# A first stage by channels: x scaled by g alone on ScalarE, its rows loaded beside the first weights

## The reference, cut to what matters

```python
def mixer_layer(h, mix_norm_g, w_in, ...):
    hn = rms_norm(h, mix_norm_g)
    proj = hn @ w_in            # h: 16 meta tokens, then x: 1024 tokens of 1024 channels
    rq, rk, rv, rg, sq, sk, sv, gr, gs = jnp.split(proj, split_points, axis=-1)
    ...
    return merged @ w_out
...
h = h + mixer_layer(h, ...)
hn = rms_norm(h, mlp_norm_g[layer])
h = h + jnp.square(jax.nn.relu(hn @ w_up[layer])) @ w_down[layer]
```

## Time and profile before

| | |
|---|---|
| median of three runs | 1614.77 us (1614.22 to 1615.44) |
| the profiled execution | 1615.03 us, its span 1613.1 us |
| PE / DVE / ACT / POOL busy | 1603.3 / 1038.1 / 769.6 / 425.7 us |
| DMA over the span | 157 GB/s |

### The profile page before, as it was taken

The page is one execution under the profiler, slowest core; times in us unless marked ns, Lnnn a source line. Parts: engine busy times, 40 slices in busy tenths (PEclk is TensorE's granted clock), DMA queues, the critical chain, the costliest instruction groups (busy, mean ns, idle before and its releaser), DMA issues.

```text
span 1613.1 us, 22668 instructions
## 1 busy us (share of the span) xinstructions
PE 1603.3 (99%) x7984; PEld 1340.3 (83%) x7984; DVE 1038.1 (64%) x1977; ACT 769.6 (48%) x1567; POOL 425.7 (26%) x611
## 2 busy tenths in 40 slices
PE   8999999999999999999999999999999999999999
PEld 6888888888888888888888888888888888888887
DVE  6775556655657787766554338866665656766675
ACT  6533334544547777762122126655555544444442
POOL 1001010221238898874211000122112222100000
PEclk9999999999999999999999999999999999999999
DMA  8323231645436566668553223354444389633452
GB/s 282 125 97 117 98 124 66 239 149 190 163 110 159 158 176 167 159 159 267 167 187 111 66 78 118 126 174 151 144 144 155 120 316 358 240 96 98 153 180 92
DMA packets 128815, 253.31 MB, mean 157 GB/s; under 512 B 14928, under 2 KB 50176, under 8 KB 128704
## 3 DMA queue, kind: packets, MB, share of 16 engines
q1 hardware_dynamic: 82656, 124.81, 24.8%
q0 software_dynamic: 45904, 126.93, 23.5%
q10 hardware_dynamic: 144, 0.13, 0.0%
HBM read 157.05 MB, written 69.47 MB: 140 GB/s over the span
## 4 chain that ended last, share of the span: by engine, by line
PE 93%; DMA 2%; DVE 2%; POOL 1%; ACT 1%; issue 0%; SPq 0%; DVEq 0%; ACTq 0%
PE bank L1089 29%; PE bank L1094 28%; PE bank L1093 28%; PE bank L1375 2%; PE bank L1407 1%; PE bank L1389 1%; DMA RT<-YA 1%; DMA XCH<-in_x_ch 0%; POOL PR L966 0%; PE bank L1132 0%; PE bank L1507 0%; PE bank L1293 0%; PE bank L1424 0%; PE bank L1457 0%; DVE WL L2177 0%; PE bank L1411 0%
## 5 line engine op out<-in xcount | busy, mean ns | idle before, releaser
L1089 PE MATMUL bank<-WH,ADH 128*128 128x512 f32 x448 | 174.3, 389 | 0.0
L1093 PE MATMUL bank<-WH,ADL 128*128 128x512 f32 x448 | 174.3, 389 | 0.0
L1094 PE MATMUL bank<-WL,ADH 128*128 128x512 f32 x448 | 174.3, 389 | 0.0
L1089 PE MATMUL bank<-HN,WH 128*128 128x512 f32 x384 | 152.9, 398 | 0.1
L966 POOL TENSOR_SCALAR PR<-PR,RC 128x272 f32<-128x272 f32 (+1 forms) x128 | 139.3, 1228 | 47.4 <-DVE RC L2672 47.2
L2103 ACT CAST ADH<-ARAW 128x512 fp32r<-128x512 f32 x112 | 69.5, 621 | 169.9 <-PE bank L1094 156.7
L1094 PE MATMUL bank<-HN,WH 128*128 128x512 f32 x384 | 150.2, 391 | 0.0
L1093 PE MATMUL bank<-HN,WL 128*128 128x512 f32 x384 | 150.1, 391 | 0.0
L2926 DVE TENSOR_TENSOR ADL<-ARAW,ADH 128x512 fp32r<-128x512 f32 x112 | 77.5, 692 | 97.1 <-ACT ADH L2103 97.1
L1089 PE MATMUL bank<-SOPH,WH 128*128 128x512 f32 x256 | 99.8, 390 | 0.0
L1093 PE MATMUL bank<-SOPH,WL 128*128 128x512 f32 x256 | 99.6, 389 | 0.0
(11 more groups left out here) (356 smaller groups left out, 4200.6 us busy)
## 6 DMA issues: line engine op xcount, KB each, us to landing
ARAW<-uop SPq DMA_DIRECT2D x112, 256.0 KB, 3.1
uop<-US POOLq DMA_DIRECT2D x64, 256.0 KB, 2.8
WRAW<-in_w_up SPq DMA_DIRECT2D x15, 1024.0 KB, 6.3
PW<-PR SPq DMA_DIRECT2D x56, 272.0 KB, 3.0
RAW<-in_w_in SPq DMA_DIRECT2D x58, 256.0 KB, 4.1
gates<-TB POOLq DMA_DIRECT2D x48, 256.0 KB, 2.7
uop<-UA POOLq DMA_DIRECT2D x48, 256.0 KB, 3.2
proj<-SA POOLq DMA_DIRECT2D x36, 256.0 KB, 2.5
```

The costliest lines, as they stand in the source:

```text
L1089: mm = pe.matmul(bank, ahi, bhi, start=first, stop=False, skip_group_check=onto)
L1093: pe.matmul(bank, alo, bhi, start=False, stop=False, skip_group_check=onto)
L1094: return pe.matmul(bank, ahi, blo, start=False, stop=last, skip_group_check=onto)
```

## The change

The first stage is rebuilt. Each norm factor belongs to a token, so it can be applied to the product's rows instead of to x. Blocks 0, 1 and 2 (FIRST = 3) now go to PE as x's channels times g alone: ACT scales four tiles of 128x128 into XGH (`hi_xg`, an activation with g as scale per partition), DVE makes the low part XGL from XCH, g and XGH (`lo_xg`), and the factor comes in when the finished bank is copied (`evict_first`, scale = RSTD). Blocks 0 and 1 share PE in pairs of steps, block 2 follows, then 3 to 7 as before. All eight blocks are still scaled for HN and SR, in the order SEQ = 3, 4, 5, 6, 7, 0, 1, 2, for which the channels of blocks 0 to 2 are loaded a second time. The eight transposes of g, `keep_x` and the transposes of blocks 0 and 1 are gone. Factor rows stand after the steps given in ROWS. The squares go in the order STAT. The loads of x's rows are all POOL's, the first four as soon as the first high part is made (`pool.wait_ge(hn_hi, 1)`); g's load goes to ACT's queue, and SP loads halves of x's channels of blocks 0 and 1 between the weights. The first sums follow the loop.

```diff
+FIRST = 3
+SEQ = (3, 4, 5, 6, 7, 0, 1, 2)
+STAT = (3, 4, 0, 5, 1, 2, 6, 7, NB)
...
         # SP
+            LATE_XG = {1: (1, 0), 3: (0, 1), 4: (1, 1)}
+            load_xg(0, 0)
             load_slab(0, w_cols(w_in, 0))
+            sp.dma_start(XCH[:, 2, :, :], x_ch[2]).then_inc(xc_full[2], 16)
+            for p in range(NB):
+                if p < 3:
+                    sp.wait_ge(hn_lo, max(XG_AT[p, 0], XG_AT[p, 1]))
+                else:
+                    sp.wait_ge(xs_rdy, 2 * (p - 2))
+                sp.dma_start(XCH[:, p % 3, :, :], x_ch[SEQ[p]]).then_inc(xc_full[p % 3], 16)
             sp.dma_start(GBC[0:META, :], g_mix[0:META, :]).then_inc(g_full, 16)
...
         # POOL
-            pool.wait_ge(w_ready, 3)
-            load_x(2)
+            pool.wait_ge(hn_hi, 1)
+            for i in range(4):
+                load_x(i)
             pool.dma_start(COLS[:, :, :], c_cols[:, 0:4 * HR].rearrange("p (a h) -> p a h", a=4)).then_inc(c_full, 16)
...
+            load_x(4)
+            load_x(5)
             store_rq(0)
+            load_x(6)
+            store_rq(1)
             load_x(7)
-            store_rq(1)
+            store_rq(2)
             load_x(8)
...
         # PE
+            keep_warm(4)
+            for pair in range(KT // 2):
+                for b in range(2):
+                    for k in (2 * pair, 2 * pair + 1):
+                        first_step(b, k)
+            ROWS = {(2, 1): 0, (3, 0): 1, (3, 5): 2, (4, 3): 3, (5, 1): 4, (5, 6): 5, (6, 4): 6, (7, 2): 7}
+            for b in range(2, NB):
+                if b == 4:
+                    pe.wait_ge(a_free, 1)
+                elif b > 4:
+                    pe.wait_ge(a_free, b - 1)
+                for k in range(KT):
+                    first_step(b, k)
+                    if (b, k) in ROWS:
+                        factors_row(ROWS[b, k])
+                    if (b, k) == (6, 6):
+                        transpose_meta()
+            pe.wait_ge(hn_lo, lo_at(1, 1))
...
         # ACT
+            def hi_xg(b, u):
+                if u == 0 or b < 2:
+                    act.wait_ge(xg_full(b, u), 16)
+                if (b, u) == XG_SEQ[0]:
+                    act.wait_ge(gc_full, 16)
+                for k in range(4 * u, 4 * u + 4):
+                    hi = act.activation(XGH[:, b, k, :], XCH[:, b, k, :], ACT.Copy, scale=GCH[:, k:k + 1])
+                hi.then_inc(hn_hi, 1)
...
+            hi_xg(0, 0)
             split_hi(0, 0, first=True)
             split_hi(0, 1, first=True)
+            hi_xg(1, 0)
+            split_hi(0, 2, first=True)
+            split_hi(0, 3, first=True)
+            hi_xg(0, 1)
+            split_hi(0, 4, first=True)
+            hi_xg(1, 1)
             for k in range(5, KT):
                 split_hi(0, k, first=True)
+            hi_xg(2, 0)
+            hi_xg(2, 1)
+            square_x(0)
+            square_x(1)
+            hi_x(3)
+            square_x(2)
+            evict_first(0)
+            square_x(3)
+            hi_x(4)
+            square_x(4)
+            evict_first(1)
+            square_x(5)
+            evict_first(2)
+            hi_x(5)
+            square_x(6)
+            evict_first(3)
+            hi_x(6)
+            square_x(7)
+            evict_first(4)
+            hi_x(7)
+            square_x(8)
+            evict_first(5)
+            hi_x(0)
+            hi_meta()
+            hi_x(1)
+            evict_first(6)
+            for k in range(4):
+                st_hi(0, 0, k)
+            hi_x(2)
+            evict_first(7)
...
         # DVE
+            def lo_xg(b, u):
+                dve.wait_ge(hn_hi, XG_AT[b, u])
+                for k in range(4 * u, 4 * u + 4):
+                    lo = dve.scalar_tensor_tensor(out=XGL[:, b, k, :], in0=XCH[:, b, k, :], scalar=GCH[:, k:k + 1],
+                                                  in1=XGH[:, b, k, :].bitcast(F32), op0=ALU.mult, op1=ALU.subtract)
+                lo.then_inc(hn_lo, 1)
...
+            invert(3)
+            dve.wait_ge(raw_full[3], 32)
+            factors(3)
+            for p in range(NB):
+                scale_x(p)
+                if p == 2:
+                    invert(2)
+                if p < 4:
+                    invert(SEQ[p + 1])
+                if p < NB - 1:
+                    factors(SEQ[p + 1])
+                lo_x(SEQ[p])
+                if p < 2:
+                    invert(p)
+                elif p == 4:
+                    invert(NB)
+                    norm_meta()
+                elif p == 6:
+                    for k in range(4):
+                        st_lo(0, 0, k)
+            for b in range(4, NB):
+                first_sum(b)
```

More of the change, by code:

```diff
@@ L57 @@
 START = 1
+FIRST = 3
+SEQ = (3, 4, 5, 6, 7, 0, 1, 2)
+AT = {b: p for p, b in enumerate(SEQ)}
+STAT = (3, 4, 0, 5, 1, 2, 6, 7, NB)
+STAT_AT = {b: p for p, b in enumerate(STAT)}
+MAKE_META = 5
 ORD = (0, 1, 4, 2, 5, 3, 6, 7)
@@ L582, in build @@
         pst_a, pst_b, PSA0, PSB0 = out_done, h1_ld, 16 * 12 * NSG, 16 * 4 * NSG
-        rt_full, RT0 = x_full, 32
-        kv_full, KV0 = x_full, 64
+        rt_full, RT0 = x_full, [48, 32, 32, 32]
+        kv_full, KV0 = x_full, [RT0[i] + 32 for i in range(4)]
         GS0, CF0, MU0 = 4, 48, 64
@@ L1185, in tokens @@
                 return lambda k: (pair[0][:, k, b * P:(b + 1) * P], pair[1][:, k, b * P:(b + 1) * P])
-            def bank_wait(j, loop=False):
-                if loop or j >= 2:
-                    pe.wait_ge(a_free, j - 1)
-            def dense_a(form, j, bank, f, act, slab, opening, closing, loop=True, middle=None, at=3):
-                bank_wait(j, loop)
-                for k in range(KT):
-                    mm = step(form, bank, k, f, act, slab, opening, closing)
-                    if j == 0 and k == 3:
-                        pe.wait_ge(hn_lo, 2)
-                    if middle and k == at:
-                        middle()
-                mm.then_inc(a_full, 1)
             def keep_warm(count):
@@ L2225, in _, with factors, norm_meta @@
-            norm_x(0)
-            split_lo(0, 0)
-            lo_x(0, (0,))
-            for k in range(1, 4):
-                split_lo(0, k)
-            lo_x(0, (1,))
+            def factors(b):
+                dve.wait_ge(rstd_rdy, STAT_AT[b] + 1)
+                dve.tensor_scalar(DG[:, AT[b] % 2, :], IDN[:, :], RSTD[:, b:b + 1], None, ALU.mult).then_inc(xn_rdy, 1)
+            def norm_meta():
+                dve.wait_ge(rstd_rdy, STAT_AT[NB] + 1)
+                dve.wait_ge(g_full, 16)
+                dve.scalar_tensor_tensor(out=ST[0:META, :], in0=XR[0:META, STAT_AT[NB] % 4, :], scalar=RSTD[0:META, NB:NB + 1],
+                                         in1=GBC[0:META, :], op0=ALU.mult, op1=ALU.mult).then_inc(xn_rdy, 1)
@@ new lines, in scale_x @@
+            def scale_x(p):
+                dve.wait_ge(xt_full, row_at(p))
+                dve.wait_ge(xc_full[p % 3], 16 * (p // 3 + 2))
+                for u in range(2):
+                    for i in range(4):
+                        k = 4 * u + i
+                        part = dve.scalar_tensor_tensor(out=x_cols(SEQ[p], u)[:, i, :], in0=XCH[:, p % 3, k, :],
+                                                        scalar=GCH[:, k:k + 1], in1=B[6 + p % 2][:, 0:P], op0=ALU.mult,
+                                                        op1=ALU.mult)
+                    part.then_inc(xs_rdy, 1)
```

295 lines of the change are left out of this document (116 added, 179 removed).

## The result

| | before | after |
|---|---|---|
| median (lowest to highest) | 1614.77 us (1614.22 to 1615.55, 5 runs) | 1622.10 us (1621.83 to 1623.81, 5 runs) |
| profiled execution, its span | 1615.03, 1613.1 us | 1621.83, 1620.0 us |
| meta products of the next stage (T) | 59.62 us | 65.93 us |
| second meta products | 139.64 us | 146.41 us |

After to before is 1.0047, with a 95% interval of 1.0032 to 1.0061: slower by 7.3 us, where 6.6 were forecast. The forecast of 1621.4 is 0.7 us low.

A forecast was written before the change was run, and what follows sets the result against it. PE was taken as the bound, busy in nearly all of 1613.1 us. T was 23.8 + 33.9 + 7.9 = 65.6, or +6.0; with a 0.6 stall, 1615.03 became 1621.6, median 1621.4 us, range 1614 to 1627.

The forecast's parts named there:

- The start: First stage: scaled halves of g's channels replace transposes, so PE starts near 8.2 us, about 1.1 us sooner.
- The two queues: Loads of x's rows beside the weights: both queues together at 0.385 MB/us, block 2's channels landing at 19.1 us.
- The up to 1 us: Loads beside the weights: packet-by-packet turns favour x's larger rows, the last weight 1.6 us later, the sum up to 1 higher.
- Row 0: First factor row, after block 2's high halves, square, root, reciprocal and diagonal: goes at 23.8 us.
- From row 0 to T: First stage up to the meta products: 33.9 us of PE's own work plus 7.9 us of waits.
- The wait at row 3: Factor row 3, after step (4,3): the other way takes 6.5 us against 4.35 on PE, stall 2.8 us.
- The one at row 4: Factor row 4: subtractions, scalings, cast and square take 5.95 us against 4.35 on PE, stall 1.6 us.
- Row 6: Factor row 6: meta's norm waits for GBC, issued behind the last XCH load, before the next scalings; stall 3.5 us.
- After T: Next stage: first sums follow the loop, half sum starts at T + 4.7 us, PE stalls 0.6 us for a bank.
- POOL's queue gets no turn: Rival, loads of x's rows: block 2 lands near 15 us, T = 62.3, time 1618.1 us; chance 0.20.
- both slow down to 247 GB/s: Rival, both DMA queues in the start: 8.3 instead of 5.3 us, T = 68.6, time 1624.4 us; chance 0.14.
- Faster: Rival, first stage: squares come before DVE asks, PE alone sets T at 55.7, time 1610.9 us; chance 0.11.

The follow-up runs named there:

- e2: The kernel after with GBC's load moved from behind the XCH loop to ahead of it; ratio to the kernel before 1.0029.
- e6: e4_both with DVE's four first sums back inside the loop; ratio to the kernel before 1.0018.
- e11: e10 with POOL's first four loads of x's rows going out beside the weights again; median 1620.29 us, ratio to the kernel before 1.0028.
- e4_both: The kernel after with both repairs, GBC's load early and the squares drawn ahead; median 1617.53 us, ratio to the kernel before 1.0014.
- e12_stage_loads_last: e8 with the next stage's loads put back behind the last XCH load; median 1614.16 us, ratio to the kernel before 0.9996.
- e1_rows_later: The kernel after with POOL's first four loads of x's rows held back until three weights are split; ratio to the kernel before 1.0041.
- e10: e8 with block 1's eviction one square earlier and the next stage's loads one XCH load later; median 1617.87 us, ratio to the kernel before 1.0017.
- e8: e6 with rows held back, block 1's eviction one square sooner and the next stage's loads among the XCH loads; ratio to the kernel before 1.0008.
- e3: The kernel after with squares of blocks 2, 6, 7 and meta before high parts, and their row loads ahead of two stores; ratio to the kernel before 1.0031.
- e13: e12_stage_loads_last with block 1's eviction one square earlier on ACT, ahead of block 2's square; ratio to the kernel before 0.9999.

## Why the prediction was right

The time came out within a microsecond because the two large terms were right, and two errors cancelled, which is luck.

- **The start** was forecast at 8.2 us and was 7.50. The scaling of 128x128, for which the earlier trace rows gave 0.16 to 0.41, takes 0.39 us: four of them 1.28 instead of 1.3. The upper row was the near one, as taken.
- **The two queues.** Block 2's channels were forecast to land at 19.1 and did at 17.6, as both queues together moved more than the 0.385 MB/us taken between the earlier trace rows. The queues of after from 11 to 13 us, then from 13 to 20:

```profile
q0 software_dynamic: 151, 0.55, 67.5%
q1 hardware_dynamic: 154, 0.28, 36.9%
```

```profile
q1 hardware_dynamic: 429, 1.48, 53.5%
q0 software_dynamic: 420, 1.38, 49.6%
```

  The second is 2.86 MB in 7 us, 0.409 MB/us, a little over the earlier trace rows. With both loaded, the queues moved packets in equal numbers. The Trainium skill (DMA: Bandwidth & Descriptors, "Queues, rings and completion order") has each engine go round the queues that have work, packet by packet; here the trace agrees. (That the profile's packets, of 2 to 4 KB, are the same as the page's is taken for granted.) From 11 to 13 us, with weights in SP's queue, that made two bytes of x's rows for each one of SP's (0.55 to 0.28 MB), as the rule was worked out in the prediction; from 13 to 20 the packets had about one mean size (3.4 and 3.3 KB), and the bytes were equal too. The up to 1 us that it would have added to the sum doesn't show. Row 0 was so 1.6 us sooner, 22.17 for 23.8. This is one execution, though: in the seven profiles with these loads the channels arrive between 17.1 and 20.1 us, and row 0 stands between 21.68 and 24.64, so the forecast lies within what kernels with this start do. PE had no idle in blocks 0 and 1, where I had 4 us of it: its products ran at half rate to 11 us in this execution, and the weights were less late than thought. I said it would not matter, and it didn't here; in e2, e6 and e11 PE had waits of 0.8 to 0.9 us on late weights, and row 0 was set by block 2 in these too.
- **From row 0 to T** 41.8 was forecast, 43.76 measured. PE's own work is 35.64 - 0.94 = 34.7 us (the run with both repairs), not 33.9. The steps themselves agree (31.82 to 36.17 in that run, six steps and a factor row, is 4.35 us for 4.33); of the 0.8, 0.3 lies beside the idle of 0.94 (36.17 to 41.77 is 5.60), 0.2 at meta's transposes (49.79 to 54.95 is 5.16 for 4.93), and the rest at the other factor rows and the end. The wait at row 3 is 2.80 as forecast. The one at row 4, 1.6 forecast, is 1.56 of slow clock. Row 5 has none, as forecast. Row 6 has 3.05 instead of 3.5, and then 1.53 of slow clock, which is the **step that was missing**: nowhere did I ask what an idle of 3 us does to the engine that idles.
- **After T**: the half sum starts at T + 4.6 (forecast 4.7), and the stage is 0.46 us longer (forecast 0.6).
- **Slips in the working**, all small: a factor row by the earlier trace rows is 5.71 - 8 x 0.68 = 0.27 us and not 0.25, the bytes of the earlier trace rows are 1.21 MB and not 1.23, which is 0.40 MB/us, and the terms of row 4 add up to 6.0 and not 5.95.

So the start was put 1.6 us too high and what follows it 2.0 too low. With the measured terms in place, the forecast of the profiled execution becomes 1621.6 - 1.6 + 0.8 + 1.5 - 0.45 - 0.15 = 1621.7; it took 1621.83.

Of the rivals, that POOL's queue gets no turn is excluded by the packets above; that both slow down to 247 GB/s too, by 409 GB/s. "Faster" was put to the test by e4_both and e12_stage_loads_last: its mechanism is real (with squares and GBC in time PE alone sets T, at 56.7 where I had put 55.7), but it needs the order that the change doesn't have. Its price was too rosy: 3.9 us at T measured 2.9, and in the median of the runs 0.7.

The parts of the loss at T, by the runs: the square's and GBC's lateness with the clock behind them 8.9 us, the rows beside the weights 2.2 to 3.4 in the two pairs of runs, with the clock of the first products in the former. What the change gains against them (6.3 - 8.9 - 2.2 is -4.8; in e12_stage_loads_last T is 2.9 ahead with 1.4 us of idles at factor rows left), such as the earlier start and the vanished idle of the earlier trace rows, was not taken apart by runs. Left open is how much of the 2.2 us of e1_rows_later is DMA and how much the clock, what sets how long the lower clock lasts behind an idle, and what makes the time behind T differ between executions.

## What to carry to other kernels

When a change makes one engine's input come through another engine's hand-written order, list for each product the last thing it needs and where that stands in the order: here two small things, a square behind casts and a 64 KB load behind 2.6 MB that wait for slots, cost 8.9 us, and the rows' loads 2 to 3. A fix of one such wait is to be read to the end of its ring (store, eviction, bank), since with two places per ring it comes back as the next one. And an idle of TensorE may not be paid with its length alone: behind the first products, those of 2.27 us and more cost 1.5 to 3.1 us on top here where this was measured, through the clock behind them, and none of up to 2.22 did.

## What the runs showed that was not expected

- **The price of an idle.** Idles of 2.27 (e10), 2.36 and 2.38 (e6, e8), 2.42 (e11), 2.57 (e3) and 2.80 to 3.05 us (after, e1, e2) were each followed by the lower clock. Behind the two of after it lasted some 3 us and cost 1.56 and 1.53. Behind those of e3, e10 and e11, all before row 6, it lasted 6 to 7 us: row 6 to T took 12.03, 12.04 and 12.02 us where e4_both takes 8.92, so 3.1 us, more than the idle itself. That doesn't go by the idle's length (behind 2.36 and 2.38 us, in e6 and e8, it was 3 to 4 us of slow clock), and what decides it is open. One of 2.22 (e3, at 40.72), those of 1.74 and 1.85 in block 2 (e4, e6) and those from 0.68 to 1.50 at factor rows were not followed by it.
- **At the start no order was found.** Behind the warming products and an idle of 1.4 to 2.0 us, the first products came at full rate in the profiles of six kernels, at half rate in five, and in e13 fell to it at the fourth, in no order of the idle's length: 1.49 us in e10 slow, 1.49 in e12 fast. Factor row 0 is 0.9 to 1.1 us later for it, where nothing else holds it (21.11 and 21.38 to 20.25).
- **The granted clock of a row can be wrong there.** In after (its stretch and its PE timeline) 9 to 12 us shows a clock of 1.00 while its products have a length of 0.63 us; with 0.39 elsewhere. In e13, where the clock from 9 to 12 us is given as 0.54, products have this same 0.63 us, so in after too it was the lower clock. The length of a product is the surer sign.

```profile
9.00:12.00 3.00, 3.00 (x11) 2.40 (x10) 2.94 (x8) 3.00 (x10) 0.64 (x2) 1.00 1.04 404
```

```profile
9.77 0.63 PE L1135 MATMUL bank<-WL,XGH 128*128 128x512 f32 x1
```

- **A store is as slow as the traffic it meets.** A 256 KB store of rq landed in 2.3 us at best, and the slowest ones took 6.6 to 7.3 us with weights streaming beside them (e8, e10, e11). The transfers that "DMA has free" for are free only if nothing small and urgent goes the same way.
